# First attention turned: a pass for maxima by queries, then scores with keys over partitions

## The reference

```python
def forgetting_attention(q, k, v, fg_logit):
    log_f = jax.nn.log_sigmoid(fg_logit.astype(jnp.float32))
    cum = jnp.transpose(jnp.cumsum(log_f, axis=1), (0, 2, 1))
    for start in range(0, S, Q_BLOCK):          # Q_BLOCK = 128
        end = start + Q_BLOCK
        qb, kb, vb = q[:, start:end], k[:, :end], v[:, :end]
        s = jnp.einsum('bqhd,bkhd->bhqk', qb, kb).astype(jnp.float32) * ATT_SCALE
        s = s + cum[:, :, start:end, None] - cum[:, :, None, :end]
        s = jnp.where(ki <= qi, s, NEG)
        p = jax.nn.softmax(s, axis=-1).astype(vb.dtype)
        outs.append(jnp.einsum('bhqk,bkhd->bqhd', p, vb))
```

## Time and profile before

| | us |
|---|---|
| median of 3 runs | 3182.46 (3180.16 to 3183.06) |
| the profiled execution | 3180.62 |
| its span, first to last instruction | 3178.8 |
| attention, first score to first product of w_out | 191.44 (332.18 to 523.62) |
| w_out, to the addition after its last product | 89.02 (523.62 to 612.64) |
| granted clock, mean of the span | 0.967 |

### The profile page before, as it was taken

The page is one execution under the profiler, slowest core; times in us unless marked ns, Lnnn a source line. Parts: engine busy times, 40 slices in busy tenths (PEclk is TensorE's granted clock), DMA queues, the critical chain, the costliest instruction groups (busy, mean ns, idle before and its releaser), DMA issues.

```text
span 3178.8 us, 33245 instructions
## 1 busy us (share of the span) xinstructions
PE 2978.6 (94%) x13804; PEld 2422.2 (76%) x13804; DVE 1433.6 (45%) x1804; ACT 1027.9 (32%) x1472; POOL 338.0 (11%) x256
## 2 busy tenths in 40 slices
PE   7988888999999999899999999999887999999996
PEld 5777566888888888778877777777766888888874
DVE  5774564454444454533234443554444223233335
ACT  3312553232222131322245555555342121111123
POOL 2212000100000000110012222022220000000003
PEclk9988999999999999999999999899998999999997
DMA  3213341211111111235423333453531111112113
GB/s 101 74 66 103 100 107 35 85 47 40 53 47 50 50 40 57 70 133 179 165 68 107 107 107 100 116 159 106 184 99 53 39 54 46 54 37 63 41 58 128
DMA packets 85125, 264.46 MB, mean 83 GB/s; under 512 B 10728, under 2 KB 13416, under 8 KB 84976
## 3 DMA queue, kind: packets, MB, share of 16 engines
q1 hardware_dynamic: 73296, 220.36, 22.3%
q0 software_dynamic: 11680, 41.98, 3.6%
HBM read 209.84 MB, written 52.46 MB: 83 GB/s over the span
## 4 chain that ended last, share of the span: by engine, by line
PE 74%; DVE 9%; ACT 6%; issue 4%; DMA 1%; POOL 1%; DVEq 0%; SPq 0%; ACTq 0%; POOLq 0%
PE ps L205 72%; ACT PB L170 2%; PE ps L208 2%; DVE cacc L176 2%; DVE YA L173 1%; DVE PB L185 1%; ACT AH L170 1%; DMA tab<-in_alibi 1%; ACT wh L170 1%; DVE PB L176 1%; POOL ga L173 1%; DVE AL L173 1%; POOL wl L173 0%; DVE AL L176 0%; DVE small L196 0%
## 5 line engine op out<-in xcount | busy, mean ns | idle before, releaser
L205 PE MATMUL ps<-AH,wh 128*128 128x512 f32 (+1 forms) x2240 | 896.5, 400 | 66.8 <-DVE AL L176 26.1
L205 PE MATMUL ps<-AL,wh 128*128 128x512 f32 (+1 forms) x2240 | 880.8, 393 | 0.0
L205 PE MATMUL ps<-AH,wl 128*128 128x512 f32 (+1 forms) x2240 | 880.1, 393 | 0.0
L173 DVE TENSOR_TENSOR wl<-raw,wh 128x1024 fp32r<-128x1024 f32 (+2 forms) x240 | 268.8, 1120 | 832.6 <-ACT wh L170 832.3
L205 PEld LDWEIGHTS ps<-AH,wh 128*128 128x128 f32 (+1 forms) x2240 | 424.2, 189 | 178.1 <-DVE AL L176 38.2
L170 ACT ACTIVATE wh<-raw 128x1024 fp32r<-128x1024 f32 (+2 forms) x289 | 261.7, 906 | 780.0 <-PE ps L205 768.1
L205 PEld LDWEIGHTS ps<-AH,wl 128*128 128x128 f32 (+1 forms) x2240 | 423.9, 189 | 92.4
L205 PEld LDWEIGHTS ps<-AL,wh 128*128 128x128 f32 (+1 forms) x2240 | 424.9, 190 | 85.4
L205 PE MATMUL ps<-UH,wh 128*128 128x512 f32 x880 | 345.5, 393 | 12.5 <-DVE wl L173 7.5
L205 PE MATMUL ps<-UL,wh 128*128 128x512 f32 x880 | 344.2, 391 | 0.0
L205 PE MATMUL ps<-UH,wl 128*128 128x512 f32 x880 | 343.8, 391 | 0.0
(11 more groups left out here) (175 smaller groups left out, 3136.3 us busy)
## 6 DMA issues: line engine op xcount, KB each, us to landing
raw<-in_w_up SPq DMA_DIRECT2D x44, 512.0 KB, 3.4
raw<-in_w_gu SPq DMA_DIRECT2D x44, 512.0 KB, 3.4
raw<-in_w_w2in SPq DMA_DIRECT2D x32, 512.0 KB, 4.2
raw<-in_w_down SPq DMA_DIRECT2D x56, 256.0 KB, 2.6
raw<-in_w_down SPq DMA_DIRECT2D x32, 320.0 KB, 2.8
xin<-in_xT SPq DMA_DIRECT2D x16, 512.0 KB, 4.4
stk<-scr_k SPq DMA_DIRECT2D x32, 256.0 KB, 6.5
stk<-scr_ka SPq DMA_DIRECT2D x32, 256.0 KB, 8.5
```

What stands on the lines that cost most here:

```text
L173: return Issued(self, self.e.tensor_tensor(out, a, b, op))
L205: return Issued(self, self.e.matmul(out, l, r, start=start, stop=stop))
```

## The change

The first attention is computed in two passes.

*Maxima.* For each head and query block (unit u = 8h + 7 - i, so the longest first) `most` multiplies the stack of q by `kh` alone and adds the mask; DVE's `maxes` takes minus the maximum of score - cum, now written back over its own input in PSUM, into one column of `mlow`. After eight, `max_halves` splits the 8 columns in high and low part in `mc` (128 x 128), PE turns `mc` (`most_rows`), and `max_rows` multiplies the rows by a selection (`C_SEL`) into rows 64 to 127 of a fourth tile of the stack, `qm`, whose rows 0 to 63 are the high part of q.

*Turned scores.* For a block of keys `kb`, in the order `KB1` = 0, 7, 1, 6, 2, 5, 3, 4, `step` makes k stationary and moves the queries from kb on: `kh` by `qt`, `kl` by `qm`, and the mask. `kl` has the low part of k in rows 0 to 63 and ones in rows 64 to 127, so minus the maximum comes in by the same product. ACT's `exps` reads PSUM, takes `cum` of the keys as its bias (a column, `cumcol`, made in stage `a` by eight small products) and writes `PTT`, in the form that the values need: nothing is transposed, and no sums are taken. `value` moves `PTT` by 128 columns of V: 64 of the head and, beside them, a column of ones (`V1` now has 65 columns per head), so that one row of the result is the sum. All key blocks of a head add up in `pair(3)`.

*Sums.* ACT copies `pair(3)` to `YS`. POOL sends the row of sums to scratch and back as 128 x 8 (`scol8`), DVE takes the reciprocal (`inverse`), POOL sends it back and loads it on 64 partitions (`RBc`), and DVE multiplies (`share`). This is done one to two heads behind.

The maxima of head h + 1 are made during head h; those of head 0 in stage `a`, between the products of v and of the convolution. There are three stacks instead of two, and head 1's is loaded before the weights of w_out.

*w_out.* The parts are taken in the order 6, 7, 4, 5, 0, 1, 2, 3. The first two tiles run seven parts each, then the last part of both. The high and low part of the second tile's weights are made at the end of attention.

Cut to its core:

```diff
+    KB1 = [0, 7, 1, 6, 2, 5, 3, 4]
+    MOST_AT = [0, 1, 2, 3, 4, 4, 5, 5]
+    def most(self, q, u):
+        h, i = u // 8, 7 - u % 8
+        q.wait_ge(S.mx, u if i >= 3 else u - 1)
...
+            q.wait_ge(S.qmr, h)
+        out = self.most_out(u)
+        for c in range(0, i + 1, 4):
+            w = min(4, i + 1 - c)
+            m = q.mm(out[:, c * 128:(c + w) * 128], qt[:, i * 128:i * 128 + 128], kh[:, c * 128:(c + w) * 128], True,
+                     c + w <= i)
+        q.mm(out[:, i * 128:i * 128 + 128], self.idR[:, :], self.maskR[:, :], False, True).then_inc(S.sc)
...
+        def step(n):
+            h, kb = n // 8, self.KB1[n % 8]
+            q.wait_ge(S.qmr, h + 1)
+            q.wait_ge(S.pwo, min(n, 1) + 1)
+            q.wait_ge(S.tex, n - 1)
+            for c in range(kb // 4, 2):
+                at = slice(max(kb * 128, c * 512), c * 512 + 512)
+                q.mm(out, kh[:, ks], qt[:, at], True, False)
+                i = q.mm(out, kl[:, ks], qm[:, at], False, c > kb // 4)
+                if c == kb // 4:
+                    i = q.mm(self.pair(n % 2)[:, ks], self.maskR[:, :], self.idR[:, :], False, True)
+        def value(n):
+            q.wait_ge(S.tex, n + 1)
+            q.wait_ge(S.tyc, h)
+            for c in range(kb // 4, 2):
+                i = q.mm(self.pair(3)[:, cols], v[:, at:at + 128], self.PTT[n % 4][:, cols], kb == 0,
+                         kb == (3, 4)[c])
+        for n in range(66):
+            if n < 64:
+                step(n)
+                for u in self.units_at(n):
+                    self.most(q, u)
+            if n >= 2:
+                value(n - 2)
+            if n % 8 == 6 and n < 56:
+                self.most_rows(q, n // 8 + 1)
...
     def dve_att1(self, q):
+        for n in range(64):
+            h, s = n // 8, n % 8
+            for u in self.units_at(n):
+                self.maxes(q, u)
+            if s == 2 and h >= 2:
+                share(h - 2)
+            if n >= 28 and n % 16 == 12:
+                mixed((n - 28) // 16)
+            if s == 5:
+                if h < 7:
+                    self.max_halves(q, h + 1)
+                if h:
+                    inverse(h - 1)
+            if s == 6 and h < 7:
+                self.max_rows(q, h + 1)
+        self.w_low(q, TILE["wout", 1])
+        share(6)
+        inverse(7)
+        share(7)
+        mixed(3)
...
+    def pool_att1(self, q):
+        for h in range(8):
+            q.wait_ge(S.tyc, h + 1)
+            q.dma(self.io["s_sum"][h:h + 1, :], self.YS[h % 2][row:row + 1, :]).then_inc(S.dsum, 16)
+            q.dma(self.scol8[:, 0:8], self.io["s_sum"][h:h + 1, :].rearrange("o (p c) -> (o p) c", c=8)).then_inc(S.dsum, 16)
+            q.wait_ge(S.yrc, h + 1)
+            q.dma(self.io["s_inv"][h:h + 1, :].rearrange("o (p c) -> (o p) c", c=8), self.scol8[:, 8:16]).then_inc(S.dinv, 16)
+            q.dma(self.RBc[a:a + 64, :], self.io["s_inv"][h:h + 1, :].to_broadcast([64, NTOK])).then_inc(S.dinv, 16)
...
     def pe_out1(self, q):
+        order = [6, 7, 4, 5, 0, 1, 2, 3]
+        for n in range(2):
+            for half in range(2):
+                self.half_product(q, s + n, self.Ah, self.Al, 8, half, 2 * n + half, P, ready, order[0:7], True, False)
+        for n in range(2):
+            for half in range(2):
+                self.half_product(q, s + n, self.Ah, self.Al, 8, half, 2 * n + half, P, ready, order[7:], False, True)
```

More of the change, by code:

```diff
@@ L405, in w_ready, with half_product @@
         return self.wh[:, s % 2, 0:TILES[s][2]], self.wl[:, s % 2, 0:TILES[s][2]]
-    def half_product(self, q, s, hi, lo, nk, half, b, m=P, ready=None):
+    def half_product(self, q, s, hi, lo, nk, half, b, m=P, ready=None, ks=None, first=True, last=True):
         h, l = self.w_ready(q, s)
         out, c = self.bank(b)[0:m, :], HALF[half]
-        for k in range(nk):
+        ks = list(range(nk)) if ks is None else ks
+        for k in ks:
             if ready:
@@ L626, in pe_a @@
                 i.then_inc(S.lnm)
+                q.wait_ge(S.cum, 1)
+                for kb in range(8):
+                    i = q.mm(self.bank(3)[:, 8 * kb:8 * kb + 8], self.cumr[0:8, kb * 128:kb * 128 + 128],
+                             self.ident[0:8, 0:8], True, True)
+                i.then_inc(S.lnm)
             if kc == 3:
@@ L1048, in act_att1, with exps @@
-        for t in range(67):
-            if 0 <= t - 2 < 64:
-                copies(t - 2)
-            if t < 64:
-                exps(t)
-            if t >= 4 and t % 2 == 0:
-                taken(t - 3)
+        def exps(n):
+            h, kb = n // 8, self.KB1[n % 8]
+            q.wait_ge(S.tsc, n + 1)
+            q.wait_ge(S.tpv, n - 3)
+            q.wait_ge(S.cuc, 1)
+            q.act(self.PTT[n % 4][:, kb * 128:], self.pair(n % 2)[:, kb * 128:], ACT.Exp,
+                  bias=self.cumcol[:, 8 * kb + h:8 * kb + h + 1]).then_inc(S.tex)
@@ new lines, in taken, with high @@
+        def taken(h):
+            q.wait_ge(S.tpv, 8 * h + 8)
+            q.wait_ge(S.mxl, 2)
+            q.wait_ge(S.yn, h - 1)
+            if h > 1:
+                q.wait_ge(S.dsum, 32 * h - 48)
+            q.act(self.YS[h % 2][:, :], self.pair(3), ACT.Copy).then_inc(S.tyc)
+        def high(tl):
+            q.wait_ge(S.yn, 2 * tl + 2)
+            q.act(self.Ah[tl], self.YT1[:, :], ACT.Copy).then_inc(S.mxh)
+        for n in range(66):
+            if n < 64:
+                exps(n)
+            if n >= 9 and n % 8 == 1:
+                taken((n - 9) // 8)
+            if n >= 27 and n % 16 == 11:
+                high((n - 27) // 16)
+            if n == 60:
+                self.w_high(q, TILE["wout", 1])
@@ L1068, in shares, with inverse @@
-        def shares(u):
-            p, m = self.PB1[u % 3][:, 0:(u % 8 + 1) * 128], self.mxc[:, (u % 3) * 4:(u % 3) * 4 + 4]
-            q.wait_ge(S.ex, u + 1)
-            q.recip(m[:, 3:4], m[:, 2:3]).then_inc(S.step)
-            q.wait_own()
-            q.ts(p, p, m[:, 3:4], None, ALU.mult).then_inc(S.nm)
-        def copies(u):
-            for n, c, w in self.blocks(u % 8 + 1):
-                n += self.CUM1[u]
-                if n % 2:
-                    self.turned_copy(q, self.PT1[u // 2 % 2], n, c, w, (u % 2) * 128, u // 2 - 1)
+        def inverse(h):
+            q.wait_ge(S.dsum, 32 * h + 32)
+            if h:
+                q.wait_ge(S.dinv, 32 * h - 16)
+            q.recip(self.scol8[:, 8:16], self.scol8[:, 0:8]).then_inc(S.yrc)
@@ L1661, in na_geo, with blocks @@
     @staticmethod
+    def blocks(nb):
+        return [(i, c, min(4, nb - c)) for i, c in enumerate(range(0, nb, 4))]
+    @staticmethod
     def na_geo(j):
@@ L2635, in layout @@
     c[:, C_EPS] = EPS
+    for j in range(8):
+        c[64 + j, C_SEL + j] = c[96 + j, C_SEL + j] = 1.0
     a["cst"] = c
```

320 lines of the change are left out of this document (191 added, 129 removed).

## The result

The changed kernel takes 3140.59 us (median of four runs, 3136.66 to 3144.37), the kernel before 3181.31 us (four runs, 3178.93 to 3183.06). The ratio is 0.9872, with a 95% interval of 0.9855 to 0.9889. The forecast was 3140 us, with a range of 3124 to 3165. The profiled execution took 3136.66 us with a span of 3134.8, against 3180.62 and 3178.8 before: 44.0 us less, where the sum had said 42.0. From median to median it is 40.7 us less, since the profiled execution is the fastest of the four.

A forecast was written before the change was run, and what follows sets the result against it. The prediction took attention to be bound by a ring of waits, some 53 us, not PE's work. w_out ending at 570.6 instead of 612.6 gave -42.0 us: 3138.6 profiled, plus 1.8 for the median, 3140 us, range 3124 to 3165.

The forecast's parts named there:

- (1): Work taken out of attention: 36 transposes, 3.7 us of PE per head, their 12 copies, accumulator reads, shares and reciprocals per block.
- (2): Work put into attention: passes for maxima, 3.4 us per head; PE's sum is 17.5 us per head, as much as before.
- (3): Attention, per head: VectorE 10.2 us and ScalarE 7.7 us, both far under PE's 17.5; 0.2 us charged for edges.
- (4): POOL's sums in attention: four chained DMAs per head at 2.5 us each; the chain fits up to 4.0 us each.
- (5): Ahead of attention PE gets 5.4 us, first step 335.2 instead of 332.2; then a 3.2 us stall and 1.7 us of clock.
- (6): Attention takes 141.8 us from 335.2, so it ends at 477.0 instead of 523.6.
- (7): w_out: head 7's 15.3 us tail hides under 19.3 us of products; PE waits 4.6 us for third-tile weights; ends at 570.6.
- A: Waits remain in attention through uneven steps and VectorE's queue order: 19.5 us per head, 3156 us; chance 0.17.
- B: POOL's chain sets the head's length in attention and the kernel is slower: 3196 us at 6 us per DMA; chance 0.06.
- C: POOL's DMAs in attention and at its tail wait for VectorE's operations running beside them: 3160 us; chance 0.06.
- D: Better: the lead-in hides the added work ahead of attention altogether and w_out's late tile costs less: 3126 us; chance 0.07.
- E: Attention's ring isn't shortened, since the next head's maxima still gate the scores: within 0.2% of now; chance 0.02.

The follow-up runs named there:

- doubled maxima: The changed kernel with the products of the pass for maxima issued twice for heads 1 to 7, without their masks: 3153.35 us, ratio 0.9904.
- doubled chain: The changed kernel with each of POOL's four DMAs per head issued twice, the second after the first has landed: 3186.89 us, ratio 1.0015.
- lighter PE work: The changed kernel with only the diagonal block of key blocks 1 and 2 multiplied in the value products: 3133.75 us, ratio 0.9842.
- the products once or twice: The changed kernel with head 0's maxima products, ahead of attention, issued once as they stand, or twice: 3141.68 us for twice, ratio 0.9871.

## Why the prediction was right, and where not

**The bound before.** Right: waiting, not PE. The kernel before runs the same products 18 us faster when one VectorE operation per block is left out.

**(1), (2) PE's work.** The mechanism was right, the size 4% too high: 17.0 us per head where I had 17.5 and 0.2 for edges. Products of 512 columns stood at 0.26 us each from four in a row. That divides by four a distance that starts and ends with a change of stage; inside a row they are closer. The time line of PE in the changed kernel has them so:

```profile
393.34 1.14 PE L206 MATMUL ps<-stk,stk 128*128 128x512 f32 x4
394.32 0.22 PE L206 MATMUL ps<-maskR,idR 128*128 128x128 f32 x1
394.38 1.30 PE L206 MATMUL ps<-PT,V 128*128 128x128 f32 x4
```

Four in 394.32 - 393.34 = 0.98, so 0.245 with the entry, over 18 such products 0.3 us per head. And the mask costs 394.38 - 394.32 = 0.06; I took 0.11 from one that stands behind a product of 128 columns, and nearly 0.09 for the others. Twelve of a head's sixteen masks cost 0.06, which makes some 0.4 us. Together that is the miss, 0.7 us per head. The doubled maxima say the same: 2.2 us for a priced 2.5. Values at 0.107 for 128 columns held, with V 128 wide.

**(3) Who could make PE wait.** Nobody did, as forecast: 0.1 us of idle PE per head. The maximum written to PSUM costs what it cost to SBUF. The group of 1024 columns, and the reads of the accumulator:

```profile
L186 DVE CUSTOM_DVE_ANT_0 ps<-ps,nck 128x1024 f32<-128x1024 f32 x7 | 8.6, 1233 | 11.5 <-PE ps L206 11.5
...
L186 DVE DVE_READ_ACCUMULATOR2_ANT small<- 128x1 f32 x56 | 7.5, 134 | 0.2
```

In the kernel before the first took 1218 ns with the output in SBUF, the second 83 ns. The lower end of that term was right, with 0.05 us per block that no row of before could show. The lag of two steps, which the forecast took for granted, is worth 10 us.

**(4) POOL's chain.** I took 2.5 us for each transfer. The medians to landing are, from 350 to 440 us, and then from 445 to 500:

```profile
RBc<-scr_inv POOLq DMA_DIRECT2D x4, 256.0 KB, 5.9
scr_sum<-YS POOLq DMA_DIRECT2D x5, 4.0 KB, 3.9
scol<-scr_sum POOLq DMA_DIRECT2D x5, 4.0 KB, 1.9
scr_inv<-scol POOLq DMA_DIRECT2D x4, 4.0 KB, 3.0
...
RBc<-scr_inv POOLq DMA_DIRECT2D x3, 256.0 KB, 3.3
scr_sum<-YS POOLq DMA_DIRECT2D x3, 4.0 KB, 1.6
scol<-scr_sum POOLq DMA_DIRECT2D x3, 4.0 KB, 1.9
scr_inv<-scol POOLq DMA_DIRECT2D x3, 4.0 KB, 1.7
```

14.7 us for the four in the first stretch and 8.5 in the second, where I had 10 for both. With hand-overs the chain of an early head is 17.1 us, against a head of 17.0; here are the first and the last issue of one head's chain and the next head's first, from POOL's time line:

```profile
364.94 0.54 POOL L213 DMA_DIRECT2D scr_sum<-YS  x1 [23.48 <-ACT YS L171]
...
376.49 0.54 POOL L213 DMA_DIRECT2D RBc<-scr_inv  x1 [2.88 <-DMA scr_inv<-scol]
381.95 0.50 POOL L213 DMA_DIRECT2D scr_sum<-YS  x1 [4.93 <-ACT YS L171]
```

The broadcast lands 5.6 us after its issue, at 382.1, 17.1 behind the first issue. That is 2.4 us more than the four transfers, where the forecast had 1.5 for hand-overs. What the chain has to meet is the place of the share in VectorE's queue: VectorE comes to it at 382.87, 0.8 us after the landing, and for heads 1 to 3 that margin is 0.7 to 0.8 us as well. So by these rows the chain fits up to about 3.9 us for each transfer (an estimate: 3.7 and a quarter of the margin), where the forecast had 4.0. That rule was nearly right, but the transfers took 3.7 us and not 2.5, so this step stood close to the bound; the doubled chain and the lighter PE work both show what happens past it. The Trainium skill, DMA: Bandwidth & Descriptors, Anatomy of one DMA — SWDGE (gpsimd) path, gives such a transfer about 2.0 us of fixed cost and adds its bytes over 436e3 us. The 4 KB rows of the second stretch are near it (1.6 to 1.9), those of the first are up to twice that; for the 256 KB broadcast the fit would give 2.6 us, an estimate, and the rows have 3.3 and 5.9, so there the rows decide.

**(5) Ahead of attention.** This step failed in size: +3.0 forecast, +6.5 in the profiled executions. Of the 6.5, 1.3 stood there before PE ran anything of the change (VectorE's subtraction of the mean starts at 298.20 instead of 296.92). From that event to the first step it is 40.5 us; the kernel before has

```profile
296.92:332.18 35.26, 29.39 (x145) 24.50 (x143) 8.59 (x8) 17.16 (x21) 7.89 (x5) 0.95 0.13 38
```

so +5.2, and in ten other executions with the products once or twice between +4.5 and +5.8 against two of before (35.3 and 34.6). The missing 2 us are clock, by an estimate: 0.87 of 40.5 us against 0.95 of 35.3 costs 5.3 - 1.8 = 3.5 us, and I had charged none ahead of the first step. The waits gave a bit more than I took (5.9 us of PE waiting before, 2.4 after: 3.5 instead of 2.4). 5.4 (by my prices) + 3.5 - 3.5 = 5.4, near the 5.2 measured. In the executions at a clock of 0.91 the same stretch is 39.8 to 40.0 us, so +4.5 to +4.7 is what most of them show.

Behind the first step the size was right and the wait was another. The forecast had PE wait 3.2 us at the third step for the first exponential. PE waits 2.91 us just ahead of that step, in a product of head 1's maxima, and for VectorE. Here are that product and, from VectorE's time line, the low part of the last `mix` tile and head 1's first maximum behind it:

```profile
343.68 0.68 PE L206 MATMUL ps<-stk,stk 128*128 128x512 f32 x2 [2.91 <-DVE small L186]
```

```profile
341.08 1.23 DVE L174 TENSOR_TENSOR AL<-cacc,AH 128x1024 fp32r<-128x1024 f32 x1 [2.76 <-ACT AH L171]
342.33 1.23 DVE L186 CUSTOM_DVE_ANT_0 ps<-ps,nck 128x1024 f32<-128x1024 f32 x1
```

The maximum was read out at 343.62, and the first exponential had ended at 343.47. Both stood behind ScalarE's high part of the same tile, so the forecast's wait would have ended within 0.2 us of the real one: here the number came out although the step named the wrong engine. The clock from 338.70 to 357.40 is 0.91, 1.7 us lost, as charged.

**(6) Attention** came to 137.25 instead of 141.8 us: 0.7 less for each head with a pass for maxima, from (2) and (3). **(7) w_out** came to 93.85 instead of 93.6, with the wait before the third tile at 4.38 (4.6):

```profile
502.73 0.77 PE L206 MATMUL ps<-AH,wh 128*128 128x512 f32 x1 [4.38 <-DVE wl L174]
```

The tail of head 7 took 14.3 us from the start of its copy (15.3 forecast) and was hidden. The sum is only 2 us off because the misses of (5) and (6), +3.5 and -4.6, cancel, with -1.2 behind w_out. That cancelling is luck, and so is the median at 0.6 us from the forecast: the profiled execution came 2.0 us under the 3138.6 of the sum, and the median stands 3.9 above it where I had added 1.8. The mechanism doesn't rest on it, since attention alone gave 54.2 us for a forecast of 49.6.

**The clock.** The stage's granted clock went from 0.96 to 0.99, and behind head 0 no half-rate stretch fell into a head: the windows of heads 1 to 5 have 1.00. The 3 us kept open for it did not come. The Trainium skill, TensorE: Matmul & The Clock Gate, Part 4, says that transposes don't count as PE's work for the clock as products do. A full clock without them agrees with that, but no run here separates the transposes from the waits that went with them.

**The rivals.** A is excluded by PE's busy 16.89 of 17.00 us, and by the doubled maxima, which show in full. B is real and starts about where it was put; it did not decide because the early transfers took 3.7 us on average, not more. C: the transfers of head 5 ran beside

```profile
448.80:464.40 15.60, 15.49 (x72) 10.70 (x71) 7.80 (x20) 6.81 (x9) 2.18 (x4) 1.00 0.06 19
```

7.8 us of VectorE's operations, nearly the 8.1 of an early head, but with a DMA share of 0.06 where an early head has 0.52, and they landed in 1.6 to 1.9 us (3.3 for the broadcast). So the rows speak for the traffic of the stack loads and against a wait for VectorE; no run took the one away and left the other. D's two parts were no accident of the change but a matter of queue order: the last tile's wait and the lead-in give 3.2 and 2.9 us when the order is turned. E is excluded by attention's 54.2 us.

## What to carry over

When a ring of waits is cut, ask for each engine which queue place its late work holds: here the broadcast is wanted at a fixed place in VectorE's queue, and it lands only 0.7 to 0.8 us before VectorE comes to that place. Price repeated products by the distances inside a full-rate row, and write down the clock that a lead-in will run at as a term of its own. When a forecast wait comes out at the forecast size, look even so at the row that ends it. An edit of under 5 us is shown by its stretch, measured from an event beside it, since whole stages move by 2 to 4 us from one execution to the next.

## What the runs showed of the hardware

- POOL's small transfers land in 1.6 to 1.9 us (medians) where the DMA share is 0.06 to 0.10, and in 1.9 to 3.9 beside stack loads at a share of 0.5 to 0.6; the broadcast of 256 KB in 3.3 and 5.9.
- A maximum of 1024 columns costs 1.233 us into PSUM and 1.218 into SBUF; the read of the accumulator behind it 134 ns and 83 ns.
- Adding 2.5 us of products to a stretch that took 39.8 to 40.5 us at a granted clock of 0.87 to 0.91 left its length at 40.4 us, at a clock of 0.96.
- Two executions of one kernel had attention's first step 3.6 us apart and ended within 0.2 us of each other.
